# A hybrid decoder trunk: six z tiles computed in pairs of seven products ahead of the scan, and a new order inside the scan steps

## The reference

```python
proj = rms_norm(x, norm_mix) @ w_in          # float32, 1024 x 5136
lru_x, lru_gate, ssd_z, ssd_xbc, ssd_dt = split(proj)     # u, g, z, xbc, dt
u = causal_dwconv(lru_x)                                  # 4 taps
r, i = sigmoid(blockdiag(u) + ...), sigmoid(blockdiag(u) + ...)
a = exp(8 * r * log_sigmoid(lam))
hr = scan(a, sqrt(1 - a*a) * i * u)                       # linear recurrence over the tokens
y_lru = rms_norm(gelu(lru_gate) * hr)
xs, B, C = split(silu(causal_dwconv(ssd_xbc)))
y = ssd_chunked(xs, softplus(ssd_dt), -exp(a_log), B, C) + xs * d   # 8 chunks of 128 tokens
y_ssd = rms_norm(y * silu(ssd_z))
x = x + concat(y_lru, y_ssd) @ w_out
```

## Time and profile before

| | us |
|---|---|
| median of 3 runs | 1404.35 (1403.97 to 1405.66) |
| profiled execution, its own time | 1402.43 |
| profiled execution, span | 1400.6 |
| PE busy | 1365.3 |
| DVE busy | 1040.9 |
| ACT busy | 842.8 |
| POOL busy | 573.5 |
| mean granted clock of PE | 0.991 |

### The profile page before, as it was taken

One profiled execution on the slowest core, in us unless ns is written; L12 is line 12 of the kernel. 1 busy time (PEld: TensorE's weight loads), 2 busy tenths in 40 slices (PEclk: granted clock), 3 DMA queues, 4 the chain that ended last, 5 costly groups with the idle time before them and its releaser, 6 DMA issues.

```text
span 1400.6 us, 20359 instructions
## 1 busy us (share of the span) xinstructions
PE 1365.3 (97%) x6703; PEld 1122.8 (80%) x6703; DVE 1040.9 (74%) x1137; ACT 842.8 (60%) x942; POOL 573.5 (41%) x496
## 2 busy tenths in 40 slices
PE   8999999999999999899999999999999999999995
PEld 7878888888888877788888788888888888888882
DVE  7966554575655768801377899989999999999987
ACT  5446525556555477400124688788888888888874
POOL 2677844676556764757200222122222222222252
PEclk8999999999999999999999999999999999999998
DMA  5132232333332444513324899999999999999978
GB/s 208 38 100 63 86 102 78 90 115 107 100 100 70 114 114 165 195 54 118 149 115 151 323 389 394 363 351 374 381 376 389 384 390 383 392 386 395 375 268 314
DMA packets 105073, 317.21 MB, mean 226 GB/s; under 512 B 18986, under 2 KB 19898, under 8 KB 104880
## 3 DMA queue, kind: packets, MB, share of 16 engines
q1 hardware_dynamic: 94144, 296.43, 58.2%
q0 software_dynamic: 10864, 19.91, 3.8%
HBM read 295.73 MB, written 39.99 MB: 240 GB/s over the span
## 4 chain that ended last, share of the span: by engine, by line
PE 88%; DVE 5%; DMA 2%; ACT 1%; issue 1%; POOL 1%; SPq 0%; POOLq 0%; DVEq 0%; ACTq 0%
PE ps L1162 38%; PE ps L717 20%; PE ps L988 9%; PE ps L821 6%; PE ps L1149 2%; PE ps L928 1%; PE ps L1182 1%; PE ps L1070 1%; PE ps L944 1%; PE ps L755 1%; PE ps L912 1%; PE ps L905 1%; PE ps L742 1%; DMA ring_gu<-y_d 1%; PE ps L729 1%
## 5 line engine op out<-in xcount | busy, mean ns | idle before, releaser
L2305 POOL TENSOR_TENSOR GH<-raw,ones 128x512 fp32r<-128x512 f32 x77 | 97.9, 1272 | 192.5 <-PE ps L717 140.9
L2143 DVE TENSOR_TENSOR split_c<-ring_gu,split_c 128x1024 fp32r<-128x1024 f32 x132 | 155.4, 1218 | 0.1
L717 PE MATMUL ps<-XH,GH 128*128 128x512 f32 x464 | 146.5, 397 | 0.5 <-POOL GL L2312 0.5
L717 PE MATMUL ps<-XL,GH 128*128 128x512 f32 x464 | 143.1, 390 | 0.0
L717 PE MATMUL ps<-XH,GL 128*128 128x512 f32 x464 | 143.0, 389 | 0.0
L2312 POOL TENSOR_TENSOR GL<-raw,GH 128x512 fp32r<-128x512 f32 x82 | 130.7, 1594 | 28.0 <-ACT GH L1499 21.8
L1162 PE MATMUL ps<-split_c,XTH 128*128 128x512 f32 x528 | 141.3, 389 | 0.0
L1540 ACT ACTIVATE split_c<-ring_gu 128x1024 fp32r<-128x1024 f32 x132 | 132.2, 1052 | 1.2 <-PE ps L1162 0.8
L2143 DVE TENSOR_TENSOR split_b<-ring_gu,split_b 128x1024 fp32r<-128x1024 f32 x98 | 116.5, 1217 | 0.0
L1162 PEld LDWEIGHTS ps<-split_c,XTH 128*128 128x128 f32 x528 | 99.1, 188 | 20.9
L1162 PE MATMUL ps<-split_b,XTH 128*128 128x512 f32 x392 | 107.9, 397 | 1.2 <-DVE XTL L2152 1.2
(11 more groups left out here) (435 smaller groups left out, 3390.2 us busy)
## 6 DMA issues: line engine op xcount, KB each, us to landing
ring_gu<-in_moe SPq DMA_DIRECT2D x264, 512.0 KB, 5.8
ring_dn<-in_moe SPq DMA_DIRECT2D x132, 512.0 KB, 6.4
raw<-in_win SPq DMA_DIRECT2D x74, 256.0 KB, 2.7
T<-acs_d SPq DMA_DIRECT2D x16, 512.0 KB, 5.0
raw<-in_wout SPq DMA_DIRECT2D x32, 256.0 KB, 2.7
T<-in_x SPq DMA_DIRECT2D x8, 512.0 KB, 6.8
X<-in_x SPq DMA_DIRECT2D x8, 512.0 KB, 4.4
x_d<-X SPq DMA_DIRECT2D x8, 512.0 KB, 2.6
```

Of the source, the lines that this page charges most:

```text
L717: mm = pe.matmul(ps[:, bank + h, :], wp[:, w, col], x[:, kk, h * 512:(h + 1) * 512], start=(q == 0 and k == 0 and n == 0), stop=(q == 1 an ...
L2143: dve.tensor_tensor(WL[slot % HL], ring[j], WH[slot % HL].bitcast(F32), ALU.subtract).then_inc(lo_made, 1)
L2305: st.link(pool.tensor_tensor(hi, raw[:, r, :], one.to_broadcast([P, GR]), ALU.mult))
```

## The change

- Six z tiles (0 to 5) are computed ahead of the scan in three more seven-product pairs, the first three of now eight. ACT writes Silu of their sums to two staging tiles in XBB (`z_stage`), SP stores them to `z_d` (`z_store`). DVE has no convolution for them.
- z tile 6 stays in step 6 (`Z_MID`), after u and turning; z tile 7 stays in step 7.
- The order on PE in steps 0 to 6 is now u, turning, (z in step 6,) half of g, states, gates, half of g, diagonals. u always uses banks 2 and 3, g (and z 6) banks 0 and 1.
- ACT's order in a step is now turned_b, decay_exp, lru_tap, square_lru, (z_tile in step 6,) lru_gates. DVE's order in a step is unchanged.
- POOL has four splits in steps 0 to 5, SP four granules. SP loads one of them behind the decay rows.
- The waits that held the decay sums and turns of the pairs are now for the Silu of the first z pair, and the late xbc tiles use banks 2 and 0.

```diff
-PAIRS = [(4, 5), (8, 9), (10, 11), (12, 13), (14, 15)]
-X_SEQ = list(EARLY) + [j for pair in PAIRS for j in pair] + list(LATE)
+Z_PAIRS = [(0, 1), (2, 3), (4, 5)]
+X_PAIRS = [(4, 5), (8, 9), (10, 11), (12, 13), (14, 15)]
+PAIRS, NZ = Z_PAIRS + X_PAIRS, len(Z_PAIRS)
+X_SEQ = list(EARLY) + [j for pair in X_PAIRS for j in pair] + list(LATE)
 X_NTH = {j: n + 1 for n, j in enumerate(X_SEQ)}
 NP, NF, NQ = len(PAIRS), 7, 3
 TILES = [("dt", 0)] + [("xbc", j) for j in EARLY + LATE]
-Z_LAST = KT - 1
+Z_MID, Z_LAST = KT - 2, KT - 1
 for _i in range(KT):
-    TILES += [(_n, _i) for _n in ("zug" if _i < Z_LAST else "ugz")]
...
+    TILES += [(_n, _i) for _n in {Z_MID: "uzg", Z_LAST: "ugz"}.get(_i, "ug")]
...
-        x_bank = lambda i: 2 * (i % 2) if i < Z_LAST else 0
-        y_bank = lambda i: 2 - 2 * (i % 2) if i < Z_LAST else 2
-        first_next = AT["z", 0] + 2
-        CONV_BANK = {0: 5, 1: 2, 2: 0, 3: 6, 6: 4, 7: 6}
+        X_BANK, Y_BANK = 0, 2
+        first_next = AT["u", 0] + 2
+        CONV_BANK = {0: 5, 1: 2, 2: 0, 3: 6, 6: 2, 7: 0}
...
+        z_stage = lambda q: XBB[:, 2 + q, :]
...
+            def z_store(p):
+
+                for q in range(2):
+                    sp.wait_ge(z_act, 2 * p + q + 1)
+                    sp.dma_start(z_d[2 * p + q], z_stage(q)).then_inc(z_out, 16)
...
-            for p in range(1, 4):
+            for p in range(1, 3):
                 pair_loads(p)
+            z_store(0)
+            pair_loads(3)
             sp.wait_ge(sp_exp, 5)
             for rows, to in ((ACS, acs_d), (EA, ea_d)):
                 sp.dma_start(to.rearrange("c r l -> r c l"),
                              rows.rearrange("r (c l) -> r c l", l=P)).then_inc(scr_out, 16)
+            z_store(1)
+            pair_loads(4)
+            z_store(2)
+            for p in range(5, NP - 1):
+                pair_loads(p)
             pair_loads(NP - 1)
             sp.wait_ge(w_lo, NF * (NP - 1) + F_NAMES.index("a12") + 1)
             granule(FIRST_LATE)
...
+                at = AT["u", i] + 2
                 if i >= 1:
                     sp.wait_ge(y_mm, i)
                     decay_rows(i)
+                    after(at - 1)
                     factors(i)
                     sp.wait_ge(gt_mm, 2 * i)
                     blocks(i)
-                at = first_next + 6 * i
                 if i == KT - 1:
                     break
                 after(at)
-                if i < Z_LAST:
-                    sp.wait_ge(z_act, i + 1)
-                    sp.dma_start(z_d[i], TI).then_inc(z_out, 16)
-                after(at + 1)
                 if i >= 1:
                     sp.wait_ge(lru_g, i)
                     sp.dma_start(hr_d[i - 1], HRR[(i - 1) % 2]).then_inc(hr_out, 16)
-                for n in range(2, 6):
-                    after(at + n)
-                if i >= Z_LAST:
+                after(at + 1)
+                after(at + 2)
+                if i == Z_MID:
                     sp.wait_ge(z_act, i + 1)
                     sp.dma_start(z_d[i], TI).then_inc(z_out, 16)
+                    after(at + 3)
+                    after(at + 4)
 
             def lru_rows(p):
                 sp.dma_start(HRT[p], hr_d[LRU_ORDER[p]]).then_inc(hrt_in[p], 16)
             def decay_sums():
                 pe.wait_ge(more_in, 32)
                 pe.wait_ge(sp_arg, 2)
...
+            def pair_read(p, q):
+
+                if p < NZ:
+                    pe.wait_ge(z_act, 2 * p + q + 1)
+                else:
+                    pe.wait_ge(cv_x, X_NTH[PAIRS[p][q]])
...
-                    if c <= Z_LAST:
-                        pe.wait_ge(yt_done, c)
-                    else:
-                        pe.wait_ge(z_act, c)
+                    pe.wait_ge(yt_done, c)
...
-            for i in range(Z_LAST):
+            def half_project(tile, q, bank):
+                granule_mms(AT[tile] + q, bank, (0, 1)).then_inc(g_used, 1)
+
+            def step(i):
                 if i == 0:
                     pe.wait_ge(cv_x, 15)
+                    half_project(("u", i), 0, Y_BANK)
+                    half_project(("u", i), 1, Y_BANK)
+                    turn_chunk(i)
+                    half_project(("g", i), 0, X_BANK)
+                    states(i)
+                    gates(i)
+                    half_project(("g", i), 1, X_BANK)
                 else:
                     pe.wait_ge(gate_act, 2 * i)
-                project(("z", i), x_bank(i))
-                turn_chunk(i)
-                if i == 0:
-                    pe.wait_ge(cv_x, 16)
-                else:
+                    half_project(("u", i), 0, Y_BANK)
+                    half_project(("u", i), 1, Y_BANK)
+                    turn_chunk(i)
                     pe.wait_ge(g_act, i)
-                project(("u", i), y_bank(i))
-                states(i)
-                pe.wait_ge(z_act, i + 1)
-                gate_project(i)
+                    if i == Z_MID:
+                        project(("z", i), X_BANK)
+                        pe.wait_ge(z_act, i + 1)
+                    half_project(("g", i), 0, X_BANK)
+                    states(i)
+                    gates(i)
+                    half_project(("g", i), 1, X_BANK)
                 pe.wait_ge(st_upd, i + 1)
                 diagonal(i, 4)
-            for i in range(Z_LAST, KT):
-                if i == 0:
-                    pe.wait_ge(cv_x, 16)
-                wait(pe, gate_act, 2 * i)
-                project(("u", i), y_bank(i))
+
+            def last_step(i):
+                pe.wait_ge(gate_act, 2 * i)
+                project(("u", i), Y_BANK)
                 turn_chunk(i)
-                wait(pe, g_act, i)
-                wait(pe, yt_done, i)
+                pe.wait_ge(g_act, i)
+                pe.wait_ge(yt_done, i)
                 gate_project(i)
                 pe.wait_ge(gate_act, 2 * i + 2)
                 states(i)
-                if i < KT - 1:
-                    pe.wait_ge(st_upd, i + 1)
                 project(("z", i), 4)
                 pe.wait_ge(g_act, i + 1)
-                diagonal(i, x_bank(i))
+                diagonal(i, X_BANK)
+
+            for i in range(Z_LAST):
+                step(i)
+            last_step(Z_LAST)
...
+            def pair_out(p, q):
+
+                if p >= NZ:
+                    pair_tap(p, q)
+                    return
+                act.wait_ge(p_sum, sum_base + 4 * p + 2 + 2 * q)
+                if p >= 1 and q == 0:
+                    act.wait_ge(z_out, 32 * p)
+                act.activation(z_stage(q), pair(pair_banks(p)[2 * q]), ACT.Silu).then_inc(z_act, 1)
+
+            def pair_silu(p, q):
+
+                if p >= NZ:
+                    silu_tile(PAIRS[p][q])
...
-                act.wait_ge(z_out, 16 * (i + 1 if i < Z_LAST else i))
+                if i >= Z_MID:
+                    act.wait_ge(z_out, 16 * (Z_MID + 1))
...
-                z_tile(i, x_bank(i), i)
-                if i >= 1:
-                    square_lru(i - 1)
                 turned_b(i)
                 decay_exp(i)
                 lru_tap(i)
+                if i >= 1:
+                    square_lru(i - 1)
+                if i == Z_MID:
+                    z_tile(i, X_BANK, i)
                 lru_gates(i)
             for i in range(Z_LAST, KT):
...
-            for j in PAIRS[0]:
-                conv_tile(j)
...
-                for j in PAIRS[p]:
+                for j in PAIRS[p] if p >= NZ else ():
                     conv_tile(j)
...
-                at = first_next + 6 * i
-                for q in range(2):
-                    split(at + q)
-                    decays(i, q)
+                at = AT["u", i] + 2
+                split(at)
+                decays(i, 0)
+                decays(i, 1)
                 skip_term(i)
-                split(at + 2)
+                split(at + 1)
                 if i >= 1:
                     add_squares(ACCL, AA, i == 1, sq_l, accl, i)
-                for n in range(3, 6):
+                for n in range(2, 6 if i >= Z_MID else 4):
                     split(at + n)
             add_squares(ACCL, AA, False, sq_l, accl, 8)
```

More of the change, by code:

```diff
@@ L429, in build @@
         s3 = lambda t, n=P: t.rearrange("p (a n) -> p a n", n=n)
-        x_bank = lambda i: 2 * (i % 2) if i < Z_LAST else 0
-        y_bank = lambda i: 2 - 2 * (i % 2) if i < Z_LAST else 2
-        first_next = AT["z", 0] + 2
-        CONV_BANK = {0: 5, 1: 2, 2: 0, 3: 6, 6: 4, 7: 6}
+        X_BANK, Y_BANK = 0, 2
+        first_next = AT["u", 0] + 2
+        CONV_BANK = {0: 5, 1: 2, 2: 0, 3: 6, 6: 2, 7: 0}
         for p, (j1, j2) in enumerate(PAIRS):
+            if p < NZ:
+                continue
             CONV_BANK[j1], CONV_BANK[j2] = (4, 6) if p % 2 else (2, 0)
@@ L506, in pair_load @@
                 j = PAIRS[p][q]
-                sp.dma_start(w_raw(p, n), a["win"][(3 + 5 * (j // 2) + j % 2) * 2 + k]
-                             ).then_inc(w_in[p % 2], 16)
```

(49 more changed lines are left out.)

## The result

| | before | after |
|---|---|---|
| median, us | 1404.16 (4 runs, 1403.64 to 1405.66) | 1436.1 (4 runs, 1434.74 to 1438.25) |
| ratio | | 1.0227, 95% interval 1.0209 to 1.0245 |
| span of the profiled run | 1400.6 | 1435.6 |
| mean granted clock | 0.991 | 0.983 |

What follows compares the result with a forecast made beforehand. PE was taken to set the time before the change. At full clock 57.4 - 6.3 - 32.2 + 2.5 = +21.4 us; with 9.6 for the clock, +31.0, so 1435 us, range 1420 to 1446.

Steps and rivals of the forecast that it cites:

- z pairs: Ahead of the scan: three more pairs at 19.14 us of PE each, +57.4 us, other engines costed at nothing.
- rival 3: PE waits in the z pairs for high halves or sums, 1 to 3 us each: about 1441 us, chance 0.07.
- The loop: Scan steps: DVE, gates, half of g, diagonals, DVE set the step; steps 1 to 5 gain 32.2 us.
- A step at full clock: Steps 1 to 5: gates start at 26.65 us, plus 9.58 us behind them, makes 36.2 us for 42.68.
- Rival 2: Each scan mask waits for a GpSimd instruction, 3.1 us against 2.02: 1446 us with the clock, chance 0.13.
- The shorter end I gave, 35.4: Lower bound of a scan step in us, if the second mask met no GpSimd instruction and lasted about 1.22.
- The clock: Behind PE's new 4.5 us waits in six steps the clock falls: 1.6 us each, 9.6 us, bounds 0 and 19.
- Rival 1: No fall of the clock behind PE's waits in the scan: +21.4, 1426 us, chance 0.22.
- Step 0: Gates start at 224.1 in place of 230.42: a gain of 6.3 us at full clock, PE wait of 4.6.
- Step 6: Keeps its z; PE waits for Silu, then gates for L1846 on states' result: 45.2 us, a loss of 2.5.
- Queues moved past: SP's and GpSimd's queues in the scan: loads, stores and splits come in time and are free.
- Rival 4: PE stays the bound, gates at 22.2 us into a step of 31.8: 1399 us, chance 0.05.

Runs made afterwards that it cites:

- Run 3: Changed kernel with 18 PE products that add zeros to g's sums ahead of the gates in steps 0 to 5: 1430.56 us.
- run 9: Changed kernel with only step 6's GpSimd splits of z's second and g's first granule put in the order PE wants them: 1431.26 us.
- run 10: Changed kernel with masks last, a quarter of g's second half ahead of gates, step 6's z behind u, its splits in PE's order: 1397.55 us.
- run 2: Kernel before with one more DVE copy ahead of the taps of u in every step: 1407.17 us.
- run 7: Changed kernel with only step 6's GpSimd split of z's second granule moved ahead of the second difference of decays: 1437.19 us.
- runs 4: Changed kernel with 12 of the 24 matmuls of g's second half moved ahead of the gates in steps 0 to 6: 1420.48 us.
- run 6: Changed kernel with DVE's taps ahead of its masks and ScalarE's first tap ahead of its B copy in steps 0 to 6: 1411.72 us.
- run 1: Changed kernel with one more DVE copy ahead of the taps of u in every step: 1450.53 us.
- run 5: Changed kernel with states ahead of g's first half in steps 0 to 6: 1437.02 us.

## Why the prediction was right, point by point

The time was right to 1.1 us, and the mechanism in steps 0 to 5 was the one forecast. That the total came so close is in part luck. In the profiled spans, which are 35.0 us apart, steps 1 to 5 were 4.5 us better than forecast, step 6 was 5.5 us worse, and 3.9 us came behind the scan, where I had forecast nothing; the medians are 31.9 apart.

- **z pairs:** right. 19.06 us each for 19.14, no wait that wasn't there before, so rival 3 is out.
- **The loop:** right, and shown from both sides. Lengthening DVE's chain by 1.13 us lengthens the waits of steps 0 to 5 by as much in the changed kernel and moves nothing in steps 0 to 6 of the one before; shortening it (masks last) brings the step to 33.3 us.
- **A step at full clock:** forecast 36.2, measured 35.47 in step 4, the only one of steps 1 to 5 at full clock. The term that was off is the second mask, 1.33 us for my 2.02. The two masks that shared 4.05 us had GpSimd work beside them; now the mask starts 0.3 us ahead of a GpSimd split, and it is the split that takes 2.14 us where others take 1.28. Rival 2, 3.1 us for each mask, is out: in steps 2 to 5 both are 1.3. In step 1 the two together take 4.04, what they took before. The shorter end I gave, 35.4, was the better value.
- **The clock:** forecast 1.6 us in each of six steps, 9.6. Measured 2.15, 1.65, 1.62, 1.62, 0 and 1.66, together 8.7, from gates and half of g against 7.66. Run 3 shows that this is a cost apart from the wait. Rival 1, no fall, is out, but step 4 took its side, and why that one escaped is open: its wait is 3.61 us like its neighbours'.
- **Step 0:** forecast a gain of 4.7 with the clock, measured 4.2.
- **Step 6:** wrong. I had +2.5 and it was +8.0. The failing step is "Queues moved past", which costed POOL's splits as free after looking at steps 0 to 5 only. In step 6 six splits, two differences, the skip product and an add stand in one queue, in an order that fitted a PE with u between z and g. That gave a wait of 3.1 us and 1.9 us more in the matmuls behind it, most of it low clock. The last section of the prediction named this as a sign of error, "a GpSimd split, which would mean that a queue is late that I have called free", and run 9 took back 5.0 us by reordering that queue alone.
- **Behind the scan:** nothing forecast, 3.9 us measured in the spans. Most of it is longer waits in w_out, but run 10 loses 3.0 there without them, and run 2 shows 2.3 us of such a difference with nothing changed behind the scan. The cause stays open: no run here isolates it.
- **Rival 4:** its price was right and its condition false for this kernel. It gave 1399 us if gates started by 22.4 us into the step. Run 10 has its 31.96 us step and 1397.55 us. What it took was new orders on DVE and ScalarE, a quarter of a half of g moved on PE, and in step 6 z ahead of the turning and a new order on GpSimd. The pairs themselves are worth their cost: with the queues in order the kernel ends 5 us ahead of the one before.

## What to carry to other kernels

Work taken out of the engine that sets the time is worth only the distance to the next loop. Write that loop out instruction by instruction before cutting, and look for an instruction in it that the loop doesn't need (here two masks ahead of three taps): moving those gave back 24.4 of the 31.9 us that the cut had lost. Then look for the next loop, here the one through ScalarE's gates. Look at each odd step for itself. A wait taken from one item of an in-order queue can come back at the next item, as in run 7, so list all of its pieces in the order in which the consumer wants them and move them together.

## What was not expected of the hardware

A wait can cost more than its length, and its length alone doesn't tell whether it will. PE's waits of 1.3 to 2.0 us ahead of the gates had full speed behind them each time (gates 1.99 us, in before, in runs 4, 6 and 10). Those of 2.73 us and more, ahead of the gates or of z's second half, had a low granted clock behind them in all cases but three. The exceptions are the 3.61 us wait of step 4 in the changed kernel, one such wait in run 9 (its step is 35.46 us long, the other four 37.1 to 37.8), and the 3.07 us wait for z's second half in run 1.

The price of one fall was mostly 1.5 to 1.7 us and at most 2.9: z's second half took 7.39 us in the changed kernel, 8.62 in run 3, 8.52 in run 5 and 5.75 in run 1, behind the same 3.07 us wait. In the kernel before with one more DVE copy, 1.13 us more of waiting thus became 2.8 us of time.

In the output product the same kind of wait went either way at shorter lengths. Behind this wait of 1.94 us in the changed kernel the granted clock was 0.66 over the next 5 us:

```profile
625.28 0.47 PE L1022 MATMUL ps<-GH,YLH 128*128 128x512 f32 x1 [1.94 <-DVE X L2051]
```

Behind 1.82 us at that place in run 6 it was 1.00. It was 0.66 behind 2.32 us in run 10 and 2.44 in run 2, and 1.00 behind 2.27 us in the changed kernel and 2.56 in before. What decides it between 1.9 and 3.6 us is open.
